# Scan steps over four head pairs, with the first scores and the first substitution placed in the value projection

## The chip, the cores and the metric

One core of one Trainium2 chip runs the whole program. The metric is the device time in microseconds, the median of several runs. Its engines are named as in the profile: PE is TensorE, DVE is VectorE, ACT is ScalarE, POOL is GpSimd and SP is SyncE, which issues most transfers.

## What is computed

A decoder of two layers over 512 tokens of width 1024, in fp32. Layer A is RWKV-7 time mixing, layer B differential attention; each is followed by a squared-ReLU MLP and a gated per-layer embedding. The change concerns only the recurrence of layer A, over 16 heads of 64:

```python
def step(S, inp):
    r_t, w_t, k_t, v_t, a_t, b_t = inp
    Sa = jnp.einsum('bhvk,bhk->bhv', S, a_t)
    S = S * w_t[:, :, None, :] + Sa[..., None] * b_t[:, :, None, :] + v_t[..., None] * k_t[:, :, None, :]
    y = jnp.einsum('bhvk,bhk->bhv', S, r_t)
    return S, y
...
r = xr @ w_rkvo[0]
k = xk @ w_rkvo[1]
v = xv @ w_rkvo[2]
```

The kernel computes it in chunks of 64 tokens. Within a chunk the dependence of a token on earlier ones is a lower triangular system; it is inverted in blocks of 32 and applied as a matmul, and only a 64x64 state per head goes from chunk to chunk.

## The kernel before

**Dense parts.** Every fp32 weight is split into a high part (ScalarE, `high`) and a low part (GpSimd, `low`, line 419), and each product is three matmuls (`three`, lines 572 to 574). Weights come in blocks of 256 columns through two slots of `wraw`, `whi` and `wlo`. Blocks 0 to 3 of the twelve projection blocks `N_K + t` are the keys, 4 to 7 the receptances, 8 to 11 the values; a block is eight steps of six matmuls. Functions in `hooks` run ahead of a chosen step of a block.

**Units.** A unit is one head pair (a 128-row tile of channels, c = 0 to 7) in one chunk: 8 x 8 = 64 units, in 16 groups q of four. Before, a group is two head pairs by two chunks (`units_of`). NQ is 16 and HALF is 8. For each group:
- the scores with the decayed a-side (`b_score`, line 703): ScalarE puts the a-tiles of two heads on the diagonal of a 128-wide tile (`early_copies`, line 1280), TensorE multiplies, and for groups 0 to 7 VectorE masks the result into NL (`scored`, line 1795), for groups 8 to 15 ScalarE takes it raw (`raw_scores`, line 1331) and GpSimd masks it (line 498);
- GpSimd spreads Bbd, Kbd and Vbd (line 459), TensorE transposes them (`turn`, line 715), ScalarE takes them to Btok, Ktok and Vtok (line 1341);
- `k_score` (line 729) gives the local scores LL, which VectorE masks (line 1848);
- the 32-blocks of eight groups at a time are inverted by a recursion of 30 steps on VectorE, two passes each (lines 1804 to 1824), and the corner block by two matmuls (`lower_times` line 740, `corner` line 749) with Nbd (line 472), Xbd (line 1858) and TiT (lines 485 and 1871).

**Scan.** Two interleaved lines x = 0 and 1. One step of a line, for one unit: `values_in` (767), `state_in` (776), Zt on VectorE (1879), its transposition `z_turn` (784), Zs on ScalarE (1355), `solve` (791), Us on ScalarE (1361), `keys_in` (799), `answer` (806, 809), the new state Hs on VectorE (1890, 1893), the decayed state Hg on ScalarE (1348), the output on ScalarE (1366). There are 32 steps. The preparation of group q + 1 is cut into eight pieces (`fill`) that are written by hand between the matmuls of two steps.

**What sets the order.** All is written by hand: each engine executes its list in order and waits on semaphores. The first eight groups' inverse runs ahead of the scan; that of the other eight (`inverse_part(1, k)`) is threaded into the first 13 steps, three recursion steps at a time between `state(1, k - 1)` and Zt of x = 1. VectorE starts the whole stage after `pe_step` 8 x 16, the end of the value projection.

Of the kernel before, what the change touches and what calls it, by code (L numbers as in the profile page):

```python
# [25 lines left out]
P = 128  # L26
# [7 lines left out]
CH = 64  # L34
# [20 lines left out]
C_ROW = C_LOW + CH  # L55
C_TRS = C_ROW + 8
# [11 lines left out]
def shape_constants():  # L68
# [8 lines left out]
    c[:, C_ROW] = (i // BL) % 2  # L77
# [50 lines left out]
def trunk(nc, x, p, norm_g, mlp_w1, mlp_w2, ple_w_up, ple_w_gate, rwkv_mix, rwkv_w_rkvo, rwkv_w0, rwkv_w1,  # L128
# [5 lines left out]
    with ctx:  # L134
# [4 lines left out]
        def at(name, offset, shape, dtype=F32):  # L139
# [6 lines left out]
        ST, HIDH, HIDL, RSTD, TMP, CST = 98432, 180352, 186496, 192640, 194688, 202880  # L146
# [46 lines left out]
        inv_t = at("inv_t", W_HI + 10240, [P, BL, BL])  # L193
        inv_p = at("inv_p", W_HI + 14336, [P, 256])
        inv_d = [at("inv_d0", W_LO, [P, NB, BL]), at("inv_d1", W_LO + 34816, [P, NB, BL])]
        inv_dt = [at("inv_dt0", W_LO + 4096, [P, NB, BL]), at("inv_dt1", W_LO + 38912, [P, NB, BL])]
# [4 lines left out]
        Zt = [at(f"Zt{k}", REST + 4096 + 512 * k, [P, P]) for k in range(2)]  # L201
        Hg = [at(f"Hg{k}", REST + 5120 + 512 * k, [P, P]) for k in range(2)]
        assert REST + 6144 <= XX
        Zs = [at(f"Zs{k}", HIDH + 512 * k, [P, P]) for k in range(2)]
        Us = [at(f"Us{k}", HIDH + 1024 + 512 * k, [P, P]) for k in range(2)]
        Hs = [at(f"Hs{k}", HIDL + 1024 * k, [P, 2, P]) for k in range(2)]
        Bbd = at("Bbd", TMP, [P, QUAD, P])
        Kbd = at("Kbd", TMP + 2048, [P, QUAD, P])
        Vbd = at("Vbd", TMP + 4096, [P, QUAD, P])

# [29 lines left out]
        row2 = cst[:, C_ROW:C_ROW + 1]  # L240
# [5 lines left out]
            bd_zero bb_pre bs_mm nl_ev nl_raw nl_mask inv_lk inv_d bbd kbd vbd nbd tdg  # L246
# [25 lines left out]
        def units_of(q):  # L272

            return 2 * (q // 4), (q % 4) * P

        def chunk_of(x, k):

            return 2 * (k // 8) + x, slice((k % 8) * CH, (k % 8 + 1) * CH)

        def states(k):  # L280

            return k - k // 8 + 1

        def kept(k):

            return 6 * (k // 8) + k % 8
# [11 lines left out]
        def _(sp):  # L298
# [74 lines left out]
            for k in range(2):  # L373
                sp.wait_ge(s.y_mm[k], NQ)
            for t in range(TT):
                sp.dma_start(xtok2[:, t, :], x[0, t * P:(t + 1) * P, :]).then_inc(s.x2_in, 16)
            slot_free(N_G2)
# [27 lines left out]
        def _(pool):  # L405
# [34 lines left out]
            lows(N_K, N_V + 4)  # L440
# [1785 lines left out]
```

## Time and profile before

| | us |
|---|---|
| median of 3 runs (1749.82 to 1750.33) | 1750.26 |
| profiled execution | 1748.08 |
| its span | 1746.2 |
| TensorE busy | 1608.3 (92%) |
| VectorE busy | 788.6 (45%) |
| ScalarE busy | 636.1 (36%) |
| GpSimd busy | 638.5 (37%) |

The profile is one execution taken by the hardware profiler. Its windows give busy time by stage, its list of waits who was waited for, its timeline single instructions with start and length. Times in the text count from the start of the span. The scan and its preparation lie between 256 and 489 us.

### The profile page before, as it was taken

What the parts mean: (1) busy time and instruction counts of PE and PEld (TensorE: products, weight loads), DVE (VectorE), ACT (ScalarE), POOL (GpSimd) and SP (SyncE); (2) the same over time, 40 slices, a digit from 0 to 9 for tenths busy, and PEclk for the clock granted to TensorE, in tenths of its full rate; (3) what the DMA queues carried; (4) which work ended last, traced back from release to release, by engine and by line L of the source; (5) the groups of instructions that cost most, each with busy time, mean ns of one, the idle gap of its engine ahead of it and who ended that gap; (6) DMA issues with size and microseconds to landing.
All of it is one profiled execution on the core that took longest, in us unless ns stands there. A gap on an engine that the chain in (4) does not pass through costs nothing. (4 is left out here: it accounts for less than half of the span.)

```text
span 1746.2 us, 20826 instructions
## 1 busy us (share of the span) xinstructions
PE 1608.3 (92%) x7503; PEld 1276.4 (73%) x7503; DVE 788.6 (45%) x1241; ACT 636.1 (36%) x1063; POOL 638.5 (37%) x309
## 2 busy tenths in 40 slices
PE   4799993879989999999999979998899999999998
PEld 3566683879937878888887767765567888888877
DVE  4866948673345532013213767357545320132133
ACT  4655433445543422122224343336724221122242
POOL 4233233334322344434433425352223343344442
PEclk8899996899989999999999999998999999999999
DMA  4112200002011233322223233220002223322221
GB/s 129 58 63 73 72 25 0 2 15 98 2 48 37 84 96 101 104 96 96 96 97 103 83 112 97 73 72 25 1 24 97 96 96 108 96 96 97 96 80 65
DMA packets 123462, 127.17 MB, mean 73 GB/s; under 512 B 8316, under 2 KB 120060, under 8 KB 123384
## 3 DMA queue, kind: packets, MB, share of 16 engines
q1 hardware_dynamic: 122720, 124.90, 21.9%
q8 instruction: 48, 0.79, 0.2%
q0 software_dynamic: 288, 0.63, 0.2%
q10 hardware_dynamic: 376, 0.61, 0.1%
q14 instruction: 30, 0.25, 0.0%
HBM read 124.00 MB, written 2.12 MB: 72 GB/s over the span
## 5 line engine op out<-in xcount | busy, mean ns | idle before, releaser
L419 POOL TENSOR_TENSOR wlo<-wraw,whi 128x2048 fp32r<-128x2048 f32 (+1 forms) x111 | 506.6, 4564 | 866.4 <-ACT whi L1167 796.2
L572 PE MATMUL pb<-xh,whi 128*128 128x512 f32 x1184 | 476.2, 402 | 27.2 <-DVE xl L1669 14.6
L573 PE MATMUL pb<-xl,whi 128*128 128x512 f32 x1184 | 465.7, 393 | 0.0
L574 PE MATMUL pb<-xh,wlo 128*128 128x512 f32 x1184 | 465.5, 393 | 0.0
L572 PEld LDWEIGHTS pb<-xh,whi 128*128 128x128 f32 x1184 | 224.7, 190 | 101.0 <-issue 38.1
L1167 ACT ACTIVATE whi<-wraw 128x2048 fp32r<-128x2048 f32 (+1 forms) x111 | 209.2, 1884 | 235.7 <-PE pb L574 235.5
L573 PEld LDWEIGHTS pb<-xl,whi 128*128 128x128 f32 x1184 | 225.2, 190 | 48.0 <-issue 3.4
L574 PEld LDWEIGHTS pb<-xh,wlo 128*128 128x128 f32 x1184 | 225.0, 190 | 47.7
L572 PE MATMUL pb<-hid_h,whi 128*128 128x512 f32 x512 | 202.4, 395 | 0.0
L574 PE MATMUL pb<-hid_h,wlo 128*128 128x512 f32 x512 | 202.3, 395 | 0.0
L573 PE MATMUL pb<-hid_l,whi 128*128 128x512 f32 x512 | 202.3, 395 | 0.0
L1980 DVE TENSOR_TENSOR X<-X,pb 128x512 f32<-128x512 f32 x40 | 25.7, 683 | 297.2 <-PE pb L574 297.2
L2012 DVE TENSOR_TENSOR tmp<-pb,rstd 128x512 f32<-128x512 f32 x64 | 41.2, 686 | 208.4 <-PE pb L574 207.9
L1465 ACT ACTIVATE hid_h<-tmp 128x512 f32 (+1 forms) x64 | 39.6, 633 | 251.1 <-DVE tmp L2016 251.1
L572 PEld LDWEIGHTS pb<-hid_h,whi 128*128 128x128 f32 x512 | 96.2, 188 | 23.1
L573 PEld LDWEIGHTS pb<-hid_l,whi 128*128 128x128 f32 x512 | 96.3, 188 | 23.0
L574 PEld LDWEIGHTS pb<-hid_h,wlo 128*128 128x128 f32 x512 | 96.2, 188 | 23.0
L1435 ACT ACTIVATE tmp<-X 128x512 f32<-128x512 f32 x40 | 24.3, 628 | 128.4 <-DVE X L1980 123.6
L1985 DVE SCALAR_TENSOR_TENSOR xl<-X,PV,xh 128x512 fp32r<-128x512 f32 x48 | 52.7, 1159 | 28.9 <-ACT xh L1176 28.9
L1174 ACT ACTIVATE xh<-tmp 128x512 fp32r<-128x512 f32 x64 | 40.1, 633 | 61.3 <-DVE tmp L1680 28.4
L1669 DVE TENSOR_TENSOR xl<-tmp,xh 128x512 fp32r<-128x512 f32 x64 | 51.2, 810 | 23.4 <-ACT xh L1174 23.4
L2082 DVE RECIPROCAL tmp<-tmp 128x512 f32<-128x512 f32 x12 | 40.2, 3346 | 23.9 <-ACT tmp L1540 23.9
(275 smaller groups left out, 2032.3 us busy)
## 6 DMA issues: line engine op xcount, KB each, us to landing
wraw<-in_mlp_w_dram SPq DMA_DIRECT2D x128, 512.0 KB, 4.3
wraw<-in_rwkv_w_rkvo_dram SPq DMA_DIRECT2D x32, 512.0 KB, 4.4
wraw<-in_ple_w_gate_dram SPq DMA_DIRECT2D x16, 512.0 KB, 4.4
xtok<-in_x_dram SPq DMA_DIRECT2D x8, 512.0 KB, 6.0
wraw<-in_w_k_shared_dram SPq DMA_DIRECT2D x8, 512.0 KB, 4.0
wraw<-in_w_v_shared_dram SPq DMA_DIRECT2D x8, 512.0 KB, 4.4
wraw<-in_diff_w_q_dram SPq DMA_DIRECT2D x8, 512.0 KB, 4.0
wraw<-in_diff_w_o_dram SPq DMA_DIRECT2D x8, 512.0 KB, 4.4
```

The lines of the kernel that those rows point to most:

```text
L419: pool.tensor_tensor(wlo[:, par, rng], wraw[:, par, rng], whi[:, par, rng].bitcast(F32), ALU.subtract).then_inc(s.w_lo, 1)
L572: mm(o, wh, ah, start=first, stop=False)
L573: mm(o, wh, al, start=False, stop=False)
L574: return mm(o, wl, ah, start=False, stop=last)
L1167: A(whi[:, par, rng], wraw[:, par, rng], ACT.Copy).then_inc(s.w_hi, 1)
L1174: A(xh[:, k, :], src, ACT.Copy).then_inc(s.x_hi, 1)
L1465: A(hid_h[:, bass.ds(4 * i + 2 * h + m, 1), :], tmp[:, 2 + m:3 + m, :], ACT.Copy)\
L1669: tt(xl[:, k, :], src, xh[:, k, :].bitcast(F32), ALU.subtract).then_inc(s.x_ready, 1)
L1980: tt(X[:, c, 0:S], X[:, c, 0:S] if old is None else old, b, ALU.add).then_inc(sem, 1)
L1985: stt(xl[:, k, :], X[:, k, 0:S], vec(k, gain), xh[:, k, :].bitcast(F32), ALU.mult, ALU.subtract)\
L2012: tt(tmp[:, m, :], pb[2 * h + m][:, :], rstd[:, :], ALU.mult).then_inc(s.dense_v, 1)
L2082: dve.reciprocal(tmp[:, i % 2, :], tmp[:, i % 2, :]).then_inc(s.qk_rs, 1)
```

## The change

- A group is now four head pairs of one chunk, and one scan step takes a whole group: line x has the head pairs 2x and 2x + 1, both in one bank of PSUM, each instruction of VectorE or ScalarE on Zt, Zs, Us and the output takes both. There are 16 steps.
- Score groups 0 to 9 are computed by hooks in blocks 9, 10 and 11 of the projections, on own tiles `early`; ScalarE takes all of them raw, between its evacuations. Score groups 10 to 15 are written between the pieces of the preparation of group 0. The mask of the half that gives answers moves to GpSimd, one pass per group (`mask_answers`), that of the other half into three passes ahead of each inverse (`block_pieces`).
- VectorE's substitution for groups 0 to 7 waits for eight raw scores and for the low part of the last but one value block, no longer for the end of the projection. Its tiles lie in the slots of `wraw`, so the load of the next weight waits for them.
- The second half's recursion is threaded in by single steps, four parts per scan step, in steps 0 to 7.
- `low` of a 2048-wide weight block is two instructions of 1024.
- The stage buffer ST and those behind it lie 384 bytes higher.

```diff
         def units_of(q):
-            return 2 * (q // 4), (q % 4) * P
+            return QUAD * (q // HALF), slice((q % HALF) * CH, (q % HALF + 1) * CH)
...
             def low(n, par, rng, first):
...
+                if rng.stop == 2048:
+                    front = slice(0, 1024)
+                    pool.tensor_tensor(wlo[:, par, front], wraw[:, par, front], whi[:, par, front].bitcast(F32),
+                                       ALU.subtract)
+                    rng = slice(1024, 2048)
...
-                     5: {5: kk_spread(3)}, 6: {6: kk_spread(4), 7: kk_spread(5)}, 7: {1: kk_spread(6)}, 8: {4: kk_spread(7)}}
+                     5: {5: kk_spread(3)}, 6: {6: kk_spread(4), 7: kk_spread(5)}, 7: {1: kk_spread(6)}, 8: {4: kk_spread(7)},
+                     9: {1: two_scores(0), 5: two_scores(2)}, 10: {1: two_scores(4), 5: two_scores(6)}, 11: {5: two_scores(8)}}
...
             def solve(x, k):
                 pe.wait_ge(s.z_ev[x], k + 1)
-                if k % 2 == 0:
-                    pe.wait_ge(s.tt_ev, 2 * (k // 2) + 2)
-                mm(pb[CB[x]][:, 0:P], set_at(x, k)[4], Zs[x][:, :], start=True, stop=True).then_inc(s.u_mm[x], 1)
+                pe.wait_ge(s.tt_ev, 2 * k + 2)
+                for i in range(2):
+                    ins = mm(pb[CB[x]][:, half_of(i)], set_at(x, i, k)[4], Zs[x][:, i, :], start=True, stop=True)
+                ins.then_inc(s.u_mm[x], 1)
...
             for t in range(12):
                 n = N_K + t
-                if t == 11:
-                    act.wait_ge(s.prep, CT)
-                    act.wait_ge(s.bd_zero, 3)
+                if t == 9:
+                    act.wait_ge(s.prep, QUAD)
+                    act.wait_ge(s.dense_v, QUAD)
+                    act.wait_ge(s.x_ready, X_V + CT)
                     early_copies(0)
                     early_copies(1)
+                if 9 <= t < 11:
+                    q = 4 * (t - 9)
+                    for m in range(q, q + 4):
+                        raw_scores(m)
+                        early_copies(m + 2)
...
-            dve.wait_ge(s.pe_step, 8 * N_G2)
-
             lk = Link(dve, s.inv_lk)
...
+            def block_pieces(hf, i):
+
+                if i == 0:
+                    dve.wait_ge(s.nl_raw, HALF * (hf + 1))
+                    if hf == 0:
+                        dve.wait_ge(s.w_lo, N_V + 3)
+                    lk.mark(tt(inv_s[hf][:, :, :], NL[hf][:, :, 0:BL], dg_a, ALU.mult))
+                elif i == 1:
+                    lk(tt(inv_d[hf][:, :, :], NL[hf][:, :, BL:CH], dg_b, ALU.mult))
...
+            LATE = ((1, 2, 3), (4, 5)) + tuple((j,) for j in range(6, 27)) + ((27, 28), (29, 30))
...
+            def mask_answers(q):
+
+                pool.wait_ge(s.nl_raw, q + 1)
+                lrb = NL[q // HALF][:, QUAD * (q % HALF):QUAD * (q % HALF + 1), CH:P]
+                pool.tensor_tensor(lrb, lrb, tri_r, ALU.mult).then_inc(s.nl_mask, 1)
+                pool.wait_ge(s.nl_mask, q + 1)
```

TensorE at the end of the projections. Before, the score groups follow the last matmul of block 11 (L574); L703 is a score group, L715 a transposition.

```order
L574 MATMUL pb<-xh,wlo 128x512
L703 MATMUL pb<-St,Bbd 128x128 x4
L703 MATMUL pb<-St,Kbd 128x128 x4
L703 MATMUL pb<-St,Bbd 128x128 x4
L703 MATMUL pb<-St,Kbd 128x128 x4
```

After, two groups (L704) stand between the matmuls of a block (L596 to L598), here for the first time in block 9.

```order
L597 MATMUL pb<-xl,whi 128x512
L598 MATMUL pb<-xh,wlo 128x512
L704 MATMUL pb<-St,early_106 128x128 x4
L704 MATMUL pb<-St,early_107 128x128 x4
L596 MATMUL pb<-xh,whi 128x512
```

Ten of sixteen groups have moved ahead of the projection's end. Next, VectorE in the scan's first half. Before, six recursion passes (L1816, L1818) stand ahead of Zt of x = 1 (L1879); L1893 is a state, L1848 the local scores.

```order
L1893 SCALAR_TENSOR_TENSOR Hs_101<-pb,small,Hg_95 128x128
L1816 TENSOR_TENSOR inv_p<-inv_d_85,inv_t 128x210
L1818 TENSOR_TENSOR inv_t<-inv_t,inv_p 128x21x10
L1816 TENSOR_TENSOR inv_p<-inv_d_85,inv_t 128x220
L1818 TENSOR_TENSOR inv_t<-inv_t,inv_p 128x20x11
L1816 TENSOR_TENSOR inv_p<-inv_d_85,inv_t 128x228
L1818 TENSOR_TENSOR inv_t<-inv_t,inv_p 128x19x12
L1858 TENSOR_TENSOR Xbd<-pb,cst 128x8x32
L1879 TENSOR_TENSOR Zt_93<-pb,cst 128x128
```

After, for the same recursion steps: L1877 and L1879 are the recursion's two passes, L1909 the local scores, L1940 Zt, L1959 the states.

```order
L1932 TENSOR_TENSOR TiT_76<-TiT_76,pb 64x4x32 x2
L1940 TENSOR_TENSOR Zt_95<-pb,cst 128x256
L1877 TENSOR_TENSOR inv_p<-inv_d_85,inv_t 128x210
L1879 TENSOR_TENSOR inv_t<-inv_t,inv_p 128x21x10
L1959 SCALAR_TENSOR_TENSOR Hs_94<-pb,small,Hg_102 128x128 x2
L1877 TENSOR_TENSOR inv_p<-inv_d_85,inv_t 128x220
L1879 TENSOR_TENSOR inv_t<-inv_t,inv_p 128x20x11
L1909 TENSOR_TENSOR LL_77<-pb,cst 128x512
L1940 TENSOR_TENSOR Zt_96<-pb,cst 128x256
```

One recursion step of two passes now stands between any two pieces of the scan. On GpSimd a group in the scan had these rows before (spreads L459, Nbd L472, diagonal blocks L485).

```order
L459 COPY Bbd<-St 64x4x64 x2
L459 COPY Kbd<-St 64x4x64 x2
L472 TENSOR_TENSOR Nbd<-NL_88,cst 128x8x32
L459 COPY Vbd<-St 64x4x64 x2
L485 TENSOR_TENSOR TiT_76<-inv_dt_86,cst 128x512
```

After, the mask of the answers (L510) is added behind the diagonal blocks.

```order
L478 COPY Bbd<-St 64x4x64 x2
L478 COPY Kbd<-St 64x4x64 x2
L487 TENSOR_TENSOR Nbd<-NL_89,cst 128x8x32
L478 COPY Vbd<-St 64x4x64 x2
L500 TENSOR_TENSOR TiT_76<-inv_dt_86,cst 128x512
L510 TENSOR_TENSOR NL_89<-NL_89,cst 128x4x64
```

Per group it is one pass more, and two passes in a row that read two inputs.

## Rows read from the trace of the kernel before

**Rows 1.** Windows: us, busy by engine (instructions), granted clock, DMA share, GB/s.

```profile
213.00:256.00 43.00, 42.51 (x186) 34.10 (x185) 22.09 (x24) 12.19 (x17) 15.25 (x6) 1.00 0.08 25
...
279.00:303.00 24.00, 3.60 (x16) 3.06 (x15) 22.25 (x54) 1.19 (x2) 1.31 (x4) 0.50 0.00 0
308.00:395.00 87.00, 70.49 (x550) 67.73 (x550) 59.66 (x142) 35.50 (x116) 31.22 (x52) 0.93 0.03 8
395.00:480.00 85.00, 84.37 (x733) 82.71 (x732) 33.33 (x99) 45.60 (x155) 33.75 (x61) 0.99 0.14 51
```

**Rows 2.** Waits of TensorE over the span: us in total, times, longest.

```profile
PE pb L740 <- DVE LL L1848: 20.8, 1, 20.8
...
PE pb L784 <- DVE Zt L1879: 16.4, 12, 2.4
```

**Rows 3.** Timeline, VectorE: start, length, instruction; local scores of groups 0, 1, 8, 15.

```profile
302.65 0.70 DVE L1848 TENSOR_TENSOR LL<-pb,cst 128x512 f32<-128x512 f32 x1
...
312.45 0.68 DVE L1848 TENSOR_TENSOR LL<-pb,cst 128x512 f32<-128x512 f32 x1
...
404.63 0.69 DVE L1848 TENSOR_TENSOR LL<-pb,cst 128x512 f32<-128x512 f32 x1 [0.15 <-PE pb L729]
...
472.49 0.69 DVE L1848 TENSOR_TENSOR LL<-pb,cst 128x512 f32<-128x512 f32 x1 [0.16 <-PE pb L729]
```

**Rows 4.** Timeline, ScalarE: the scan's last output.

```profile
489.08 0.22 ACT L1366 ACTIVATE St<-pb 128x64 f32<-128x64 f32 x1 [0.53 <-PE pb L809]
```

**Rows 5.** Timeline of VectorE and GpSimd: the first substitution, and copies beside it.

```profile
264.95 2.01 DVE L1804 SCALAR_TENSOR_TENSOR inv_t<-NL,cst 128x1024 f32<-128x1024 f32 x1
...
278.40 0.44 DVE L1816 TENSOR_TENSOR inv_p<-inv_d,inv_t 128x130 f32<-128x130 f32 x1
...
280.63 0.33 DVE L1816 TENSOR_TENSOR inv_p<-inv_d,inv_t 128x168 f32<-128x168 f32 x1
...
299.06 2.02 DVE L1822 STREAM_TRANSPOSE inv_d<-inv_t 128x1024 f32<-128x1024 f32 x1
...
277.86 0.85 POOL L459 COPY Bbd<-St 64x256 f32<-64x256 f32 x2
```

**Rows 6.** Timeline, ScalarE in the value projection: evacuations (L1299) and a weight copy.

```profile
222.51 1.09 ACT L1299 ACTIVATE St<-pb 128x512 f32<-128x512 f32 x2 [4.46 <-PE pb L574]
223.48 1.92 ACT L1167 ACTIVATE whi<-wraw 128x2048 fp32r<-128x2048 f32 x1
...
245.03 1.09 ACT L1299 ACTIVATE St<-pb 128x512 f32<-128x512 f32 x2 [7.99 <-PE pb L574]
...
255.92 1.08 ACT L1299 ACTIVATE St<-pb 128x512 f32<-128x512 f32 x2 [8.19 <-PE pb L574]
```

**Rows 7.** Timeline, TensorE: first and last of the 16 score groups.

```profile
255.72 1.06 PE L703 MATMUL pb<-St,Bbd 128*128 128x128 f32 x8
...
274.46 1.16 PE L703 MATMUL pb<-St,Kbd 128*128 128x128 f32 x8 [0.34 <-ACT Kbd L1280]
```

**Rows 8.** Timeline, TensorE: two pieces of one unit in the second half.

```profile
471.18 0.39 PE L799 MATMUL pb<-Vtok,Ktok 128*128 128x128 f32 x2
471.40 0.39 PE L767 MATMUL pb<-LL,Vtok 128*128 128x128 f32 x2
```

**Rows 9.** Groups by shape, 300 to 490 us: count, busy us, mean ns, idle before.

```profile
L485 POOL TENSOR_TENSOR TiT<-inv_dt,cst 128x512 f32<-128x512 f32 x16 | 20.6, 1290 | 67.5 <-PE pb L809 44.9 <-DVE inv_dt L1824 22.5
...
L1879 DVE TENSOR_TENSOR Zt<-pb,cst 128x128 f32<-128x128 f32 x64 | 18.6, 290 | 52.0 <-PE pb L776 43.4 <-PE pb L767 8.4
...
L1355 ACT ACTIVATE Zs<-pb 128x128 f32<-128x128 f32 x64 | 17.7, 276 | 29.2 <-PE pb L784 29.0
```

**Rows 10.** Timeline, TensorE: a transposition of Zt that waited.

```profile
353.54 0.33 PE L784 MATMUL pb<-cst,Zt 128*128 128x128 f32 x1 [1.95 <-DVE Zt L1879]
```

**Rows 11.** Timeline: a pass of VectorE beside a low part, and TensorE behind it.

```profile
1017.11 4.66 DVE L1977 TENSOR_TENSOR tmp<-tmp 128x512 f32<-128x512 f32 x1 [1.52 <-ACT tmp L1435]
...
1023.36 2.04 PE L605 MATMUL pb<-tmp,cst 128*128 128x512 f32 x2 [6.73 <-DVE tmp L1977]
```

More of the change, by code:

```diff
@@ L209, in trunk @@
         Vbd = at("Vbd", TMP + 4096, [P, QUAD, P])
+        early = [at("early0", CST + 4 * C_END + 4 * CT * NV + 896, [P, QUAD, P]), at("early1", RSTD, [P, QUAD, P])]
         hid_h = at("hid_h", ST, [P, 16, S], F32R)
@@ L438, in lows @@
                         low(n0 + 2 * i + h, (n0 + h) % 2, slice(0, 2048), False)
-            lows(N_K, N_V + 4)
+            pool.memset(early[0][:, :, :], 0.0).then_inc(s.bd_zero, 1)
+            lows(N_K, N_V + 2)
+            pool.wait_ge(s.kb_ps, CT)
+            pool.memset(early[1][:, :, :], 0.0).then_inc(s.bd_zero, 1)
+            lows(N_V + 2, N_V + 4)
             link = Link(pool, s.pool_link)
@@ L507, in _ @@
                 spread(Kbd, K_, q, s.kbd)
-                lower_block(q)
                 if q:
+                    lower_block(q)
                     pool.wait_ge(s.tr_mm, 3 * q)
-                    spread(Vbd, V_, q, s.vbd)
+                else:
+                    pool.wait_ge(s.inv_ld, 1)
+                    pool.memset(Vbd[:, :, :], 0.0).then_inc(s.bd_zero, 1)
+                    pool.wait_ge(s.pe_step, 8 * N_G2)
+                    for t in (Xbd, Nbd):
+                        pool.memset(t[:, :, :], 0.0).then_inc(s.bd_zero, 1)
+                    pool.wait_ge(s.bd_zero, 7)
+                    pool.wait_ge(s.dense_a, 36)
+                spread(Vbd, V_, q, s.vbd)
+                if q == 0:
+                    lower_block(q)
                 diagonal_blocks(q)
+                mask_answers(q)
             for k in range(2):
-                pool.wait_ge(s.y_mm[k], 2 * NQ - 2)
+                pool.wait_ge(s.y_mm[k], NQ - 1)
             low(N_G2, 0, slice(0, 2048), False)
             for k in range(2):
-                pool.wait_ge(s.y_mm[k], 2 * NQ)
+                pool.wait_ge(s.y_mm[k], NQ)
             low(N_WO, 1, slice(0, 2048), False)
@@ L811, in fill @@
+                pe.wait_ge(s.nl_mask, k + 1)
+                for i in range(2):
+                    lrb = NL[k // HALF][:, QUAD * (k % HALF) + 2 * x + i, CH:P]
+                    ins = mm(pb[ZY[x]][:, i * P + CH:(i + 1) * P], Us[x][:, i, :], lrb, start=False, stop=True,
+                             skip_group_check=True)
+                ins.then_inc(s.y_mm[x], 1)
             def fill(q, slot):
@@ L816, in fill @@
                     turn(q, 0)
+                    k_score(q, 0, 2)
                 elif slot == 1:
[L818 removed]
+                    k_score(q, 2, 4)
+                    turn(q, 1)
                 elif slot == 2:
[L820 to L827 removed]
+                    lower_times(q, 0, 4)
+                else:
                     turn(q, 2)
[L829 removed]
                     corner(q)
[L832 to L835 removed]
+            b_score(10)()
+            b_score(11)()
+            fill(0, 0)
+            b_score(12)()
+            b_score(13)()
+            fill(0, 1)
+            b_score(14)()
+            b_score(15)()
+            fill(0, 2)
+            fill(0, 3)
             values_in(0, 0)
[L837 to L839 removed]
+            for k in range(NQ + 1):
+                if k < NQ:
                     state_in(0, k)
@@ L843, in _ @@
                     keys_in(1, k - 1)
-                fill(q, f)
-                if k < 2 * NQ:
+                fill(k + 1, 0)
+                if k < NQ:
                     z_turn(0, k)
@@ L848, in _ @@
                     answer(1, k - 1)
-                fill(q, f + 1)
-                if k < 2 * NQ:
+                fill(k + 1, 1)
+                if k < NQ:
                     solve(0, k)
```

434 lines of the change are left out of this document (221 added, 213 removed).

## The prediction

> **What bounds the kernel now.** I read the stages of the span first (the windows), then who made TensorE wait, then the timelines of single engines. Over the whole span TensorE is the engine that sets the time, except in the stage this change rewrites, the chunked scan of the RWKV layer and its preparation. From 213 to 256 us, the value projection, TensorE is busy 42.5 of 43 us; from 279 to 303 us it is busy 3.6 of 24 us at a granted clock of 0.50 while VectorE is busy 22.3; from 308 to 395 us it is busy 70.5 of 87; from 395 to 480 us it is busy 84.4 of 85 [rows 1]. The two largest waits in this stage are the one of 20.8 us for the local scores LL, which stand on VectorE behind the first-half substitution, and 16.4 us in twelve pieces for Zt [rows 2]. So three prices are to be worked out: when the scan can start, what a group of four units costs in its first half (where VectorE still carries the second substitution) and in its second half, and the tail.
>
> How the scan now runs. LL(q) marks the groups: LL(1) at 312.45, LL(8) at 404.63, LL(15) at 472.49 [rows 3]. Seven groups of the first half take 92.18 us, 13.2 each; seven of the second take 67.86, 9.69 each. The last output copy ends 0.22 us after its start at 489.08, so at 489.3 [rows 4]; from LL(15) to there are 16.8 us.
>
> **Start of the scan.** Before, VectorE begins the first-half substitution at 264.95 and LL(0) stands at 302.65, 37.7 us later [rows 3, 5]. It could begin only when the value projection was over (its last evacuation is at 255.92 [rows 6]) and the first eight score groups were out. The change computes score groups 0 to 9 inside blocks 9 to 11 of the projections.
> - TensorE: a score group is 8 passes in about 0.9 us (8 x 0.11, the same kind as in rows 8; 1.06 with the last one's drain [rows 7]). Block 9 starts when block 8 ends, 222.45. Its hook at the second of eight steps (1.36 us each, a block of 10.9 us by the distance of two evacuations, 245.03 to 255.92) comes at 223.8, but the first copy into the early tile stands on ScalarE behind the evacuation at 222.51 and the weight copy at 223.48, which ends at 225.40 [rows 6], and takes 0.85. TensorE waits until 226.2, 2.4 us. Then four groups, 3.6 us: block 9 ends at 239.3. Block 10 has four groups and ends at 253.8, block 11 two groups and ends at 266.5 instead of 255.9. This delay of the projection, 10.6 us, is paid by taking ten groups out of the 16 that now stand behind it (255.72 to 275.6 [rows 7]).
> - ScalarE turns each group over in 0.60 + 0.85 us; raw score 7 is out at 250.9. By then the low part of the last weight has left GpSimd (ScalarE's copy until 242.3, then an instruction as long as the 4.66 us hold of rows 11: 247), so VectorE starts at 250.9, 14.0 us earlier.
> - The substitution itself: three passes of 1024 elements replace the one of 2.01 us: 1.25 + 1.25 + 2.2; then transposition 1.25, copy 0.7, ones 0.1 come to 6.8. Steps 7 to 30 took 18.4 us undisturbed (280.63 to 299.06 [rows 5]), steps 1 to 6 have the lengths of the last six and take 3.5 by them. Before, from 264.95 to step 7 at 280.63 it was 15.7 us, since GpSimd masked the second half against VectorE; now this part is 6.8 + 3.5, and GpSimd has only memsets and one spread of Vbd there, for which I put 1.5. The two last transpositions are 3.6. Sum 33.9: LL(0) at 284.8, 17.9 us earlier.
> - From LL(0) to the first Zt it was 5.8 us; now three passes for the second half (1.25, 1.25, 2.2) are threaded between, against diagonal and mask work on GpSimd; I take 9.2, so Zt at 294.0. TensorE works in this stretch at the low clock as it did in the 0.50 stretch before [rows 1], since it still waits some 6 us for LL(0). The first step has more of VectorE's work (transposition, copy, three and two recursion steps); LL(1) comes at 296.5 and the next step begins at 302.3. LL(1) is **16.0 us earlier** than 312.45.
>
> **A group in the second half.** The count of matmul passes per four units does not change: 12 transpositions, 24 passes of scores, lower blocks and corner, and 13 for each unit, 88 in all. Two full passes follow each other in 0.22 us [rows 8], so 72 x 0.112 + 16 x 0.09 = 9.5 us; a group now takes 10.0 (9.69 plus the two chunk ends, 1.1 us shorter each, among the seven). The rest is short waits at the head of the scan's matmuls. With two head pairs in one step there are half as many of them. Chain of one pair of heads per step: state_in 0.45, Zt 0.42 (0.29 for 128 elements, 0.69 for 512 [rows 9, 3]), transposition 0.35, Zs 0.39 (0.28 for 128 [rows 9]), solve 0.55, Us 0.39, answer 0.55, two states 0.70, eight hand-overs of 0.05: 4.2 us, well inside 9.7, and between any two links of it TensorE has 0.9 to 2.1 us of other work. The corner and Vtok are the tightest (0.9 us of corner over a copy of 0.6). I take **9.7**; bounds 9.5 and 10.0.
>
> **A group in the first half.** Three recursion steps in a row stood before one Zt: in one instance TensorE waited 1.95 us for Zt [rows 10]. Now one step (0.8 us) stands between two links. By my hand schedule of one step, from state_in(0) at 0: Zt(0) 0.74 to 1.16 with its transposition due at 2.2; states(1) until 3.8; the next recursion step meets GpSimd's diagonal pass (1.29 [rows 9]) and the new mask (half the elements, 0.7), both released at 3.3, and ends at 6.1; LL 6.8 where the lower blocks wanted it at 5.84: TensorE waits 1.0; the rest hides. 9.5 + 1.0 = **10.5**. Bounds: 9.7 (no collision counts) and 13.3, what it is now with the chunk end added back. The last recursion step and the two transpositions of the second half add 1.0 once.
>
> LL(1) to LL(15) is then 11.9 (first step) + 6 x 10.5 + the seventh step's rest and 6 x 9.7 with the chunk end of four units (-2.2) and +1.0, together 141.3 us, against 160.0: **-18.7**. Tail: LL(15) sits 5.0 us into its step, so 4.7 remain, and the last step is one chain of each x plus the wait behind the weight copy of 1.90 us that also stands there now: 7.2. 11.9 against 16.8: **-4.9**.
>
> **Low parts in halves.** GpSimd's long instructions hold VectorE: a 0.69 us pass took 4.66 at 1017.11, and TensorE then waited 6.73 us [rows 11]. In halves each hold is at most 2.3, but the second half comes right behind and meets the next VectorE pass, so I count only the one pass that slips between, 0.5 us at each of the two places where TensorE waits for it: **-1.0**. Elsewhere TensorE works through 10.9 us blocks and neither the hold nor the 0.1 us of a second instruction reaches the end; without that cover 100 such pairs would cost 10 us.
> The Trainium skill (SBUF — State Buffer, "Who interferes with whom") says that an instruction of VectorE with two SBUF inputs and one of GpSimd that reads SBUF exclude each other for the whole of an instruction; the 4.66 us row agrees with it. By that rule alone a hold would shrink by 2.3 us at each of the two places, -4.6 instead of -1.0. The tile shifts and the 384 bytes cost nothing.
>
> **Sum.** -16.0 - 18.7 - 4.9 - 1.0 = -40.6. The profiled execution took 1748.08 us (span 1746.2), 2.2 under the median: 1750.26 - 40.6 = **1710**.
>
> **Rivals.**
> - *The first half keeps its waits.* VectorE's order is still fixed; if every recursion step runs into GpSimd, a step stays at 13.3: 7 x 2.8 = +20, 1730. For it: GpSimd has 0.7 us more per group, and by the counts above VectorE's own work is 7.3 us, 9 with the holds. Against: single steps instead of three. 12%.
> - *GpSimd's copies block too.* The six spreads of 0.43 us per group could hold VectorE as the two-input passes do: +1.0 on a step by two more holds, 1717. Against: a pass of VectorE ran in 0.44 us beside such copies [rows 5]. This is what the skill's rule on that page would give, since a copy reads SBUF. 12%.
> - *Serial chains, slower.* If solve, copy and answer of both x no longer hide each other, because each link waits for two units' work, a step is 2 x 4.2 + 5.6 us of fill = 14.0: 7 x 3.5 + 7 x 4.3 = +55, 1765. It decides against the change from 12.8 us a step on. Against: the 84.4 of 85 us busy with shorter links. 5%.
> - *The early start fails.* Hooks stall on the copies of ScalarE in all three blocks, or VectorE starts only after the projection (267): +14, 1724. 6%.
> - Forecast: 65%.
>
> **Numbers.** The forecast's own bounds: 14 steps by -0.2 or +0.3 and -0.8 (first half), the start +-3: 1700 to 1716. Up to the first rival it is 1730; below 1700 and above 1728 I leave about 2 in 10. A measurement of this kernel can tell 0.2%, 3.5 us, from no change. Faster 0.94, same 0.01, slower 0.05.
>
> **What would show it.** LL(0) near 285, first Zt near 294, LL(1) to LL(8) about 10.5 apart, LL(8) to LL(15) 9.7, the projection ending at 266, the last output copy at 450. Waits for Zt should go from 16.4 to a few us, waits for LL before the lower blocks should appear, about 1 us each. Wrong would be: steps of 12 or more in the first half (rival one), or a TensorE wait over 3 us at the hooks of blocks 10 and 11.

## The result, and the profile after

The median fell from 1750.04 to 1694.99 us (four runs each; ratio 0.9688, 95% interval 0.9671 to 0.9705). That is 55 us where I had forecast 40.6, and below the low end of the range, 1700. The profiled executions took 1748.08 and 1695.06 us, their spans 1746.2 and 1693.2: 53.0 us. One remark is needed for the numbers below: the times of one kernel lie up to 9.6 us apart (before: 1741.86 to 1751.45 in 23 runs), and what differs between them is how long the granted clock of TensorE was low (mean clock 0.967 to 0.971 in the runs of before below 1744 us, 0.963 to 0.967 in those above 1749). So I give medians for the verdicts and traces for the places.

Windows of after, columns as in [rows 1]: the value projection, the substitution up to the first Zt, and the two halves of the scan.

```profile
213.00:256.00 43.00, 40.92 (x209) 33.61 (x208) 25.45 (x26) 22.16 (x38) 18.50 (x14) 1.00 0.08 25
266.00:290.00 24.00, 15.01 (x96) 13.97 (x95) 21.81 (x43) 9.70 (x20) 8.70 (x10) 0.72 0.00 1
293.00:375.00 82.00, 76.84 (x663) 74.19 (x661) 61.02 (x140) 33.15 (x91) 40.37 (x71) 1.00 0.03 9
375.00:437.00 62.00, 60.30 (x530) 58.97 (x528) 22.59 (x61) 27.82 (x77) 30.97 (x55) 1.00 0.19 69
```

The stretch in which VectorE works alone is still there, but TensorE now does 15 of its 24 us instead of 3.6, and in the first half of the scan it is busy 77 of 82 us where it was 70.5 of 87. The waits of TensorE in after answer to [rows 2]; columns: us in total, times, longest.

```profile
PE pb L772 <- DVE LL L1909: 8.3, 1, 8.3
...
PE pb L629 <- DVE tmp L2056: 5.8, 1, 5.8
...
PE pb L748 <- ACT Btok L1401: 3.8, 14, 0.3
...
PE pb L704 <- ACT early L1329: 1.9, 3, 1.2
...
PE pb L854 <- ACT Us L1421: 1.4, 1, 1.4
```

The 20.8 us for LL are 8.3, the 16.4 for Zt are 0.5. New are 14 short waits of 0.27 us for the copy of Btok. The timeline of VectorE in after: the start of the substitution, and the local scores of groups 0, 1, 8 and 15 (as [rows 3]).

```profile
249.27 1.23 DVE L1856 TENSOR_TENSOR inv_s<-NL,cst 128x1024 f32<-128x1024 f32 x1 [17.14 <-ACT NL L1334]
...
282.14 0.70 DVE L1909 TENSOR_TENSOR LL<-pb,cst 128x512 f32<-128x512 f32 x1
...
293.45 0.69 DVE L1909 TENSOR_TENSOR LL<-pb,cst 128x512 f32<-128x512 f32 x1
...
367.62 0.69 DVE L1909 TENSOR_TENSOR LL<-pb,cst 128x512 f32<-128x512 f32 x1 [0.28 <-PE pb L761]
...
436.95 0.69 DVE L1909 TENSOR_TENSOR LL<-pb,cst 128x512 f32<-128x512 f32 x1 [0.28 <-PE pb L761]
```

The last output copy of the scan (as [rows 4]), and the two last links ahead of it on TensorE:

```profile
448.91 0.71 PE L831 MATMUL pb<-Zs,TiT 128*128 128x128 f32 x4 [0.47 <-ACT Zs L1415]
450.98 1.12 PE L854 MATMUL pb<-NL,Us 128*128 128x64 f32 x4 [1.36 <-ACT Us L1421]
...
452.13 0.28 ACT L1426 ACTIVATE St<-pb 128x128 f32<-128x128 f32 x1 [1.21 <-PE pb L854]
```

Where the 53.0 us come from, by the start of the same instruction in both timelines:

| same instruction | before | after | offset | in this piece | forecast |
|---|---|---|---|---|---|
| weight copy behind block 8 | 223.48 | 221.26 | -2.2 | -2.2 | 0 |
| LL(1) | 312.45 | 293.45 | -19.0 | -16.8 | -16.0 |
| LL(15) | 472.49 | 436.95 | -35.5 | -16.5 | -18.7 |
| last output copy of the scan | 489.08 | 452.13 | -37.0 | -1.4 | -4.9 |
| a matmul of the group norm | 499.78 | 462.06 | -37.7 | -0.8 | 0 |
| one behind the norm's root | 526.64 | 486.05 | -40.6 | -2.9 | 0 |
| ahead of the first MLP's hidden rows | 631.40 | 590.96 | -40.4 | +0.2 | 0 |
| behind them | 943.11 | 897.63 | -45.5 | -5.0 | 0 |
| end of the attention projections | 1170.87 | 1124.45 | -46.4 | -0.9 | -1.0 |
| in the attention | 1234.40 | 1185.27 | -49.1 | -2.7 | 0 |
| at the second MLP's hidden rows | 1414.65 | 1365.77 | -48.9 | +0.2 | 0 |
| near the end | 1703.20 | 1649.57 | -53.6 | -4.7 | 0 |

The scan and its preparation (three rows of forecasts) gave 34.7 us instead of 39.6. Within it only the first half gained: LL(1) to LL(8) took 92.2 us and takes 74.2, LL(8) to LL(15) took 67.9 and takes 69.3. Not all of the 18.0 need be the change's: before has three stretches of 3.4 us at the low clock in that half (from 332.0, 345.7 and 393.5), after has none, and the same scan took between 88.4 and 92.2 us in the traces of the other kernels that keep it (b_stage384, b_stage128).

The excess lies behind the scan, in code of which the change touches no line but the halves, and comes in two kinds. The first is in both MLPs. Groups of instructions over the span, matmuls with the hidden activations; us busy, mean ns of one; first before, then after:

```profile
L572 PE MATMUL pb<-hid_h,whi 128*128 128x512 f32 x512 | 202.4, 395 | 0.0
L574 PE MATMUL pb<-hid_h,wlo 128*128 128x512 f32 x512 | 202.3, 395 | 0.0
```

```profile
L596 PE MATMUL pb<-hid_h,whi 128*128 128x512 f32 x512 | 199.4, 389 | 0.0
L598 PE MATMUL pb<-hid_h,wlo 128*128 128x512 f32 x512 | 199.2, 389 | 0.0
```

The 6 ns are a difference of start to start as well. Timeline of TensorE, seven matmuls apart; before 1.40 us for six, after 1.37:

```profile
1439.61 0.40 PE L574 MATMUL pb<-hid_h,wlo 128*128 128x512 f32 x1
...
1441.01 0.40 PE L574 MATMUL pb<-hid_h,wlo 128*128 128x512 f32 x1
```

```profile
1439.66 0.39 PE L598 MATMUL pb<-hid_h,wlo 128*128 128x512 f32 x1
...
1441.03 0.39 PE L598 MATMUL pb<-hid_h,wlo 128*128 128x512 f32 x1
```

Over all 1536 of them the mean distance is 233.2 and 226.8 ns: 9.8 us. The second kind is the clock. Windows behind a gap of the group norm and in the attention (granted clock is the third number from the end), before, then after, same code:

```profile
519.90:526.60 6.70, 6.07 (x13) 3.90 (x14) 2.77 (x4) 1.17 (x2) 0.00 (x0) 0.50 0.00 0
1183.00:1192.00 9.00, 8.48 (x23) 5.22 (x24) 5.67 (x16) 4.39 (x17) 1.87 (x3) 0.50 0.13 44
```

```profile
482.70:486.10 3.40, 3.28 (x14) 2.19 (x14) 2.01 (x4) 0.00 (x0) 0.00 (x0) 1.00 0.00 0
...
1136.00:1140.00 4.00, 2.76 (x10) 1.96 (x10) 3.63 (x6) 2.77 (x10) 0.66 (x1) 0.57 0.49 168
1140.00:1146.00 6.00, 6.00 (x30) 3.49 (x29) 5.32 (x16) 4.25 (x14) 1.21 (x2) 1.00 0.00 1
```

Behind the group norm the low stretch (6.8 us before) is absent; in the attention 10.2 us of it have become 3.4.

### The profile page after: what moved, and what is told of

The parts are those of the page before. It is cut to its first block and busy times, and to the rows that moved or that the text cites. A ratio compares the mean times of both kernels' runs of the same rounds, so it can differ in the third digit from the quotient of the medians.

```text
span 1693.2 us, 20697 instructions
## 1 busy us (share of the span) xinstructions
PE 1581.9 (93%) x7503; PEld 1264.5 (75%) x7503; DVE 773.1 (46%) x1205; ACT 624.3 (37%) x975; POOL 666.1 (39%) x427
## 5 line engine op out<-in xcount | busy, mean ns | idle before, releaser
L435 POOL TENSOR_TENSOR wlo<-wraw,whi 128x1024 fp32r<-128x1024 f32 x108 | 260.7, 2414 | 807.3 <-ACT whi L1214 752.2
L596 PE MATMUL pb<-xh,whi 128*128 128x512 f32 x1184 | 476.4, 402 | 28.6 <-DVE xl L1729 16.2
L598 PE MATMUL pb<-xh,wlo 128*128 128x512 f32 x1184 | 464.9, 393 | 0.0
L596 PEld LDWEIGHTS pb<-xh,whi 128*128 128x128 f32 x1184 | 224.6, 190 | 103.1 <-issue 42.0
L438 POOL TENSOR_TENSOR wlo<-wraw,whi 128x1024 fp32r<-128x1024 f32 x111 | 274.3, 2471 | 20.8 <-ACT whi L1214 20.8
L598 PEld LDWEIGHTS pb<-xh,wlo 128*128 128x128 f32 x1184 | 224.7, 190 | 47.8
L596 PE MATMUL pb<-hid_h,whi 128*128 128x512 f32 x512 | 199.4, 389 | 0.0
L598 PE MATMUL pb<-hid_h,wlo 128*128 128x512 f32 x512 | 199.2, 389 | 0.0
L598 PEld LDWEIGHTS pb<-hid_h,wlo 128*128 128x128 f32 x512 | 96.1, 188 | 20.1
L596 PEld LDWEIGHTS pb<-hid_h,whi 128*128 128x128 f32 x512 | 96.1, 188 | 19.6
```

Source lines behind the costliest of these rows:

```text
L435: pool.tensor_tensor(wlo[:, par, front], wraw[:, par, front], whi[:, par, front].bitcast(F32), ALU.subtract)
L596: mm(o, wh, ah, start=first, stop=False)
L598: return mm(o, wl, ah, start=False, stop=last)
```

## Experiments

**Undo the side changes and do them alone.** Theory A: the start address of the stage buffer sets how fast TensorE reads the hidden activations. Theory B: the halves of the low parts do it, and the 384 bytes do nothing, as I had written.

```diff
-        ST, HIDH, HIDL, RSTD, TMP, CST = 98432, 180352, 186496, 192640, 194688, 202880
+        ST, HIDH, HIDL, RSTD, TMP, CST = 98816, 180736, 186880, 193024, 195072, 203264
```

In before alone:

> Kernel before with only the six tiles from the stage buffer on moved up by 384 bytes; nothing else. Theory A (where the stage buffer starts sets how fast TensorE reads the hidden activations): the 1536 matmuls that read hid_h and hid_l stand 233.2 ns apart before and 226.8 after, so 1536 x 6.4 ns = 9.8 us less, and about 0.3 us from the low-rank ones: near 1740. The waits of the scan (20.8 us for LL, 16.4 for Zt) stay. Theory B, that of my prediction (the shift costs and brings nothing; the faster spacing comes from halves of the low parts): 1750, spacing unchanged.

Measured 1740.52 (12 runs; ratio to before 0.9957, interval 0.9938 to 0.9976): -9.8, with the distance at 226.8. The clock did not help: its median over the runs is 0.963, against 0.966 of before. The reverse in after:

> Kernel after with the six tiles put back by 384 bytes. Theory A: +10 us, 1705, the hidden matmuls 233 ns apart again, and the scan as in after (LL(1) 293.4, LL(15) 437, last output copy 452). Theory B: 1695. The two places where the granted clock was about 0.5 before and 1.00 after (520 to 527 and 1183 to 1192 us before) are watched: if the clock there has to do with when they come, the first one keeps its clock here, since nothing ahead of it moves, and the second may change.

Measured 1702.20: +4.5 to +7.2 against the two medians of after (1697.71 and 1694.99); the distance is 233.2 again. The traces tell more than these medians. The span is 8.2 us longer than that of after: the hidden rows of the two MLPs give back some 10 us by the offsets (4.7 and 5.2), and 2.3 are regained between 950 and 1080 us, where the two kernels' stretches at the low clock differ. The mean clock over the runs is a little higher as well (0.980, against 0.974 to 0.978 in those of after). The scan is as in after. Of the two places that were watched, the first keeps its full clock and the second has 3.4 us at the low one, both as in after. Theory B falls: the spacing follows the address in both directions.

**Which address.** Before with two other shifts, one run each (1742.02 and 1749.71 us; the spacing is what is compared).

```diff
-        ST, HIDH, HIDL, RSTD, TMP, CST = 98432, 180352, 186496, 192640, 194688, 202880
+        ST, HIDH, HIDL, RSTD, TMP, CST = 98560, 180480, 186624, 192768, 194816, 203008
```

> Kernel before with the six tiles up by 128 bytes in place of 384. The tile xh, whose matmuls stand 228 ns apart, starts a whole number of 512 bytes from the slab's start; the hidden tiles of before start 128 bytes past such a place, those of after on one, these 256 past one. If 256 bytes are the step that counts: spacing of the hidden matmuls 227 ns as in after. If it is 512: 233 ns as before, or something between. If any other place than that of before is good (a clash with one certain other tile): 227. One look; the spacing is read from the trace.

> Kernel before with the six tiles up by 256 bytes: 384 bytes past a multiple of 512. If steps of 256 or 512 bytes count: 233 ns. If any other place than that of before is good: 227 ns.

Groups of instructions, up by 128 bytes, then up by 256:

```profile
L572 PE MATMUL pb<-hid_h,whi 128*128 128x512 f32 x512 | 199.3, 389 | 0.0
```

```profile
L572 PE MATMUL pb<-hid_h,whi 128*128 128x512 f32 x512 | 202.3, 395 | 0.0
```

Distances 226.8 and 233.0 ns. So at 0 and 256 bytes past a multiple of 512 from the slab's start the reading is fast, at 128 and 384 it is slow: among the four places tried, multiples of 256 are good.

**Halves alone, and whole parts in after.**

```diff
+                if rng.stop == 2048:
+                    front = slice(0, 1024)
+                    pool.tensor_tensor(wlo[:, par, front], wraw[:, par, front], whi[:, par, front].bitcast(F32),
+                                       ALU.subtract)
+                    rng = slice(1024, 2048)
```

> Kernel before with only the low weight parts computed in two instructions of 1024 columns in place of one of 2048. Theory A: the spacing of the hidden matmuls stays at 233 ns; the gain is what the trace of after shows at the places where TensorE or VectorE stands behind GpSimd: 2.2 us between 180 and 221 us and 0.9 at 1023, so -3, near 1747. My prediction's term: -1.0, 1749. By the rule of a lock for a whole instruction at each of two places: -4.6, 1745.5. Theory B (halves make the spacing shorter): -12 or more, 1738.

> Kernel after with the low weight parts in whole instructions again. If halves are worth the same as alone in before, about +3: 1698. If the new order of the scan's preparation leans on them (VectorE works against GpSimd's low parts from 249 to 256 us), +4 to +6: 1700. By my prediction's term: +1.0, 1696.

Alone: 1740.72 (ratio 0.9955, interval 0.9938 to 0.9973), -9.6, more than the terms of 1.0, 3 and 4.6; and since the hidden matmuls stay 233.2 ns apart, Theory B falls here too. After without the halves: 1701.45, +3.7 to +6.5, also more than the 1.0 of my prediction. VectorE in before at the two places, first the clamp ahead of the key norm's reciprocal (here GpSimd works from 182.57 to 187.56), then the place of [rows 11]:

```profile
184.44 3.40 DVE L1734 TENSOR_SCALAR rstd<-rstd 128x512 f32<-128x512 f32 x1 [1.35 <-ACT rstd L1260]
...
1017.11 4.66 DVE L1977 TENSOR_TENSOR tmp<-tmp 128x512 f32<-128x512 f32 x1 [1.52 <-ACT tmp L1435]
...
1022.52 0.69 DVE L1977 TENSOR_TENSOR tmp<-tmp 128x512 f32<-128x512 f32 x1 [0.76 <-ACT tmp L1435]
```

With halves:

```profile
184.34 1.18 DVE L1739 TENSOR_SCALAR rstd<-rstd 128x512 f32<-128x512 f32 x1 [1.36 <-ACT rstd L1265]
...
1007.93 2.50 DVE L1982 TENSOR_TENSOR tmp<-tmp 128x512 f32<-128x512 f32 x1 [1.52 <-ACT tmp L1440]
...
1011.19 1.99 DVE L1982 TENSOR_TENSOR tmp<-tmp 128x512 f32<-128x512 f32 x1 [0.76 <-ACT tmp L1440]
```

At the place of [rows 11] the mechanism of my step holds: the first hold shrinks by 2.2, the next pass, free before, is now held 1.3, and 1.0 us is left (the wait of 6.7 becomes 5.7), where my sum had 0.5. A hold of the same length 20 us earlier (at 997.01 in before) gives nothing: its 4.77 becomes 2.56, the next pass goes from 0.68 to 2.88, and TensorE's wait behind them stays at 2.1. At the clamp the whole 2.2 us come through: TensorE's wait for that reciprocal fell from 2.7 to 0.5. Even so the 1.18 us are not free of the first half, which ends at 185.24: the same clamp takes 0.42 at 152.64 in before, where GpSimd is idle. The rest is between 1000 and 1130 us of before (990 to 1120 here), where TensorE's waits for xl fell from 6.7 us in four to 4.7 in three and one of 0.8 is gone, against two new ones of 0.3 for low parts. By offsets 2.6 us are gained up to 223 us (in it a new wait of 0.8 us for a low part, and one stretch at the low clock less) and 2.7 between 1000 and 1130 us, together 5.3. The rest of the 9.6 goes with the clock: its median over the runs is 0.971, against 0.966 of before. Whether the halves bring that about is not shown.

The reason that the expectation had for +4 to +6 in after, that the new scan leans on the halves, does not hold: the trace without them is 2.1 us behind after at 212 us and still 2.1 behind at LL(15).

The Trainium skill (SBUF — State Buffer, "Who interferes with whom") calls the hold exclusive for a whole instruction, and lists `tensor_scalar`, the clamp's operation, among those that can take the shared ports with a single input; the 3.40 us that became 1.18 agree with that where the next instruction of VectorE takes no second input from SBUF, and at the other place the second half's hold takes most of it back.

**Both together, scan as before.**

> Kernel before with both side changes: tiles up by 384 bytes and low parts in halves; the scan as before. If the two add up by the medians of the single runs (-9.8 and -9.6): 1731. By the offsets of the traces, leaving out the stretches at the low clock (-9.8 and about -6): 1734. What is left to after, 36 to 39 us, is then the scan's and its preparation's, against the 39.6 of my prediction for these.

Measured 1732.89 (ratio 0.9908, interval 0.9887 to 0.9929): -17.2. The next run, timed together with it, takes after as it is:

> Kernel after unchanged, timed with the others of this call. The runs of the kernels so far fall into two heaps some 8 us apart (before: 1742 and 1750.5), each stretch at the low clock costing TensorE 1.7 to 3.4 us. If that belongs to every variant, after has a second heap too, near 1703 or 1687; if the new scan has left fewer waits that let the clock fall, all runs stay within 2 us of 1695.

1697.71, from 1695.86 to 1700.02 in 5 runs: not 8 us apart as before is, but not within 2 either. 35.2 us by the medians are thus the new scan with its preparation, against the forecast of 39.6.

**The early scores put back behind the projection** (ScalarE's copies move with them).

```diff
-                     9: {1: two_scores(0), 5: two_scores(2)}, 10: {1: two_scores(4), 5: two_scores(6)}, 11: {5: two_scores(8)}}
...
+            for q in range(0, HALF + 2, 2):
+                two_scores(q)()
```

> Kernel after with the ten score groups taken out of blocks 9 to 11 of the projections and put behind the projection, with their ScalarE copies; all else as in after. Then the substitution starts after the projection (256) and eight score groups at ScalarE's pace of 1.45 us, near 268 in place of 249.3, and TensorE no longer loses 10.6 us in the projection. Theory: LL(1) 17 to 18 us later, 1712. Rival (what the early start gives is taken back by something else, as the two transpositions and the second half's masks): +10 or less, under 1705.

Measured 1719.49, timed together with the 1697.71 of after, so +21.8 (spans of the traces +18.2). VectorE's start and TensorE's wait in this kernel:

```profile
267.95 1.22 DVE L1850 TENSOR_TENSOR inv_s<-NL,cst 128x1024 f32<-128x1024 f32 x1 [37.42 <-ACT NL L1335]
```

```profile
PE pb L773 <- DVE LL L1903: 22.2, 1, 22.2
```

The start is 18.7 us later than 249.27 and nothing behind it takes that back. Of the 35.2 us this leaves 13 to 17 for all the rest of the new scan, the steps of four head pairs, the threading and the masks together; no kernel with the steps alone taken out was run.

**Recursion steps in threes.** My reason for the shorter first half was that one recursion step, no longer three, stands ahead of a Zt.

```diff
                     local_scores(k + 1)
+                    if k:
+                        for i in range(4 * k - 2, 4 * k + 1):
+                            inverse_late(i)
                     z_spread(1, k)
...
-                    inverse_late(4 * k)
```

> Kernel after with the second substitution's steps of a scan step put together again: three in a row ahead of the second Zt (as before the change), one behind the states, in place of four single ones between the links. My prediction ascribes the waits of TensorE for Zt in the first half (16.4 us in 12 before) to this grouping: three steps of 0.8 us in a row put each Zt some 1.6 us late, six to seven steps of the scan: +8 to +11 us on the 10.65 us period (12 and more), about 1706. Rival: two head pairs per step give TensorE enough other work beside each Zt, and the grouping does not matter: within 2 us of 1697, period 10.7.

Measured 1697.08, as after (1697.71 and 1694.99, neither timed together with it). LL comes every 10.58 us (303.71 to 346.01 in four groups) against 10.65. Window 316 to 345 us of this kernel, then of after, and this kernel's waits for Zt:

```profile
316.00:345.00 29.00, 28.02 (x245) 27.24 (x244) 20.21 (x50) 12.10 (x34) 14.12 (x25) 1.00 0.01 1
```

```profile
316.00:345.00 29.00, 28.01 (x244) 27.14 (x243) 21.34 (x51) 11.48 (x32) 13.35 (x24) 1.00 0.01 1
```

```profile
PE pb L823 <- DVE Zt L1940: 1.9, 3, 1.2
```

Within those 29 us TensorE is busy 28 in both. In these steps the grouping costs nothing: the waits for Zt are 0.1 to 0.2 us each. Only at 360.8 us does TensorE wait 1.2 for a Zt, and a stretch of 3.4 us at the low clock follows; with it LL(1) to LL(8) takes 75.7 us against 74.2. That the second head pair gives TensorE the work that covers three recursion steps is the likely reason; no run separates it. So it is not the single steps that took the waits for Zt away, as I had it.

**The second half.** A group takes 10.29 us (385.51 to 436.95 in five), more than before's 10.0. TensorE and ScalarE of after in one such group: the copy of Btok starts behind the answers (L854), which have nothing to do with it.

```profile
415.28 0.56 PE L854 MATMUL pb<-NL,Us 128*128 128x64 f32 x4
415.68 0.66 PE L761 MATMUL pb<-St,Kbd 128*128 128x128 f32 x4
416.61 0.66 PE L748 MATMUL pb<-cst,Kbd 128*128 128x128 f32 x4 [0.27 <-ACT Btok L1401]
```

```profile
415.96 0.60 ACT L1401 ACTIVATE Btok<-pb 128x512 f32<-128x512 f32 x1 [2.09 <-PE pb L854]
```

ScalarE waits for `y_mm`, since the set is free only when its last reader is done; of Btok itself the last reader is the matmul ahead (L848, `h_mm`).

```diff
                 if q >= 2 and i == 0:
-                    act.wait_ge(s.y_mm[0], q - 1)
-                    act.wait_ge(s.y_mm[1], q - 1)
+                    for x in range(2):
+                        act.wait_ge(s.h_mm[x], q - 1 - (q - 1) // HALF)
```

> Kernel after with two waits of ScalarE changed. (1) Its copy of the turned Bbd into Btok waits for the matmuls that read the old Btok, no longer for the answers behind them (0.45 us later). TensorE waits 0.27 us per group for that copy, 14 times, 3.8 us in all: -3.8 if that wait is what keeps the group at 10.29 where I had forecast 9.7. (2) The weight copy of 1.90 us at the end of the scan goes behind the last Us copy: TensorE waited 1.36 us there: -1.4. Sum -5, about 1690. Rival: another link takes the wait's place (the period stays above 10.2): -1.4 alone, 1693.6. If the period comes to 10.0, not 9.7, it is TensorE's own 88 passes that set it.

Measured 1694.98, timed together with the 1697.71 of after: -2.7. The Btok wait is gone from the list; LL comes every 9.89 us (387.99 to 437.46 in five), and TensorE is busy all of those 49.47 us. The wait for the last Us went from 1.36 to 0.47. The 88 passes alone thus take 9.9, where I had 9.5 and 0.2 for waits.

The first half did not get shorter: its groups stay at 10.6 to 10.7 us although TensorE no longer waits for Btok there. In its place TensorE waits 0.45 to 0.58 us in each of five groups ahead of the lower blocks (L772). The profile names no releaser ("issue"), but each of these waits ends 0.1 us after LL does (LL starts at 347.73 and takes 0.69). In after the same waits are there, behind those for Btok: 0.06 to 0.17 us in five groups, 0.87 in the seventh.

```profile
348.53 1.05 PE L772 MATMUL pb<-inv_d,Nbd 128*128 128x32 f32 x8 [0.47 <-issue]
```

What is still lacking in the sum is partly clock. The profiled run is one of the two slowest of five (1698.55). By offsets against the second trace of after its scan gains 0.8 us, and a fall of the clock takes 3.0 in it; without that fall the two waits give 3.9 of the 5. In the seventh group TensorE had stood 0.27 and later 0.87 us in after; here it stands 1.27 at once, for LL(7), and the clock falls, as it does in the next kernel, which has the same pause. The row of this kernel, then its window:

```profile
359.93 1.05 PE L772 MATMUL pb<-inv_d,Nbd 128*128 128x32 f32 x8 [1.27 <-issue]
```

```profile
361.70:368.50 6.80, 6.80 (x35) 6.80 (x35) 5.09 (x7) 1.59 (x4) 0.93 (x3) 0.52 0.00 1
```

**Is it the standing that lets the clock fall?** In all 13 other traces, before's included, the clock falls in two waits of TensorE. Here they are filled with work that nothing reads, where TensorE waits 5.8 us for a norm's sum and 4.3 us for the head norms:

```diff
+                for _ in range(n):
+                    mm(pb[bank][:, :], ones, cst[:, 0:S], start=True, stop=True)
...
+                busy(7, 6)
                 norm_total(4)
...
+            pe.wait_ge(s.lg, 64)
+            busy(0, 4)
```

> The kernel with the two changed waits of ScalarE (1695.0 median, period 10.02), and added work that nothing reads: six 128x512 matmuls of constants on TensorE where it waits 5.8 us for the key norm (976 us in after), four where it waits 4.3 us for the head norms (1216 us). In both places the granted clock then falls to 0.50 for 6.8 us, while TensorE has full work. Theory: the clock falls because TensorE stood idle; with the gap filled it stays at 1.00 there, and each place gives 3.4 us less the small delay of the fillers: -6, 1689 (against 1695.0 of that kernel). Rival: the clock falls anyway, or somewhere else soon after: 1695 or up to 2 us over it.

Measured 1689.00 (1686.94 to 1692.84; ratio to before 0.9666, interval 0.9643 to 0.9688): -6.0 against the 1694.98 of the kernel it is built on (not timed together; before had 1750.08 beside the one and 1750.04 beside the other), and faster than both before and after. Windows over the two gaps, with the added work, then in the second trace of after:

```profile
970.00:983.00 13.00, 12.46 (x43) 7.70 (x42) 8.02 (x4) 3.42 (x5) 8.62 (x3) 1.00 0.32 93
1211.00:1225.00 14.00, 12.77 (x35) 6.16 (x36) 9.76 (x11) 5.59 (x8) 0.00 (x0) 1.00 0.00 1
```

```profile
971.00:984.00 13.00, 7.12 (x17) 4.72 (x16) 6.52 (x3) 3.93 (x5) 8.60 (x3) 0.74 0.28 90
1212.00:1227.00 15.00, 9.47 (x29) 4.74 (x29) 5.76 (x5) 4.91 (x7) 0.00 (x0) 0.77 0.00 0
```

Each of the two falls is gone. By the starts of the same instructions this kernel leads that trace by 1.6 us at 978 and by 4.5 at 990, by 4.5 at 1200 and by 6.8 at 1228: 2.9 and 2.3 us. In these two places the clock fell because TensorE stood, and keeping it busy with work that nothing reads gives the time back. The other falls stay: those at 361.7 and 959.1 us, for instance, are in this trace as in that of the kernel it is built on (362.0 and 962.8).

## Why the prediction was wrong, point by point

- **The stage buffer.** The step that failed first: "the tile shifts and the 384 bytes cost nothing". I asked only what a shift could break, found nothing, and put down zero on both sides. It is worth 9.8 us by the spacing (233.2 to 226.8 ns, 1536 times), seen in both directions. That alone would have moved the forecast to 1700. All six tiles moved together in every such run; the spacing that was compared is that of the matmuls which read the hidden activations. The profile of before held the hint: by groups, the same shape of matmul took 395 ns with hid_h and hid_l and 389 with xl and wlo in the same MLP.
- **The low clock behind the scan.** The sum carried the stretches of before at the low clock along as if they belonged to the code. One of them was absent in after and one was shorter, 2.9 and 2.7 us, and the medians differ by 2 us more than the two profiled executions. These are not shown to be the change's: the same wait of 2.9 us ahead of the group norm is followed by a fall in before and in the kernel with the two changed waits, and by none in after, in its second trace and in the kernel with the added work. The range had no term for it.
- **Halves.** -1.0 was sized for two places at 0.5. The place of [rows 11] alone gave 1.0 and the hold at 997 us nothing; the key norm's clamp (2.2) and the other waits between 1000 and 1130 us were not looked for. After against after with whole parts is 3.7 to 6.5 us; the Trainium skill's rule at two places, -4.6, was nearer in size, though not for its reason.
- **Start of the scan.** Right in mechanism and size: -16.8 against -16.0, and 18.7 us when undone. In detail, the hook of block 9 stalled 1.2 us, not 2.4; VectorE began at 249.3 (forecast 250.9), LL(0) came at 282.1 (284.8), LL(1) at 293.5 (296.5). Of these leads 2.2 us were there before block 9, from the halves (the two traces spend the same 31 us at the low clock up to 210 us, in different pieces). The parts listed for LL(0) add to 33.8, not 33.9.
- **First half.** 10.65 against 10.5. The term for LL had the right mechanism: TensorE does wait for LL ahead of the lower blocks, about 0.5 us instead of 1.0 once the wait for Btok is gone (in after 0.1 behind Btok's 0.27), and taking the wait for Btok away did not shorten these groups. But what is left of a group is 10.1 to 10.3 us, where I had 9.5, so that 10.5 came so near is luck. My reason for the end of the waits for Zt was wrong: with three recursion steps in a row the period is 10.58.
- **Second half.** 10.29 against 9.7, outside my bounds of 9.5 to 10.0 and the reason why LL(1) to LL(15) gave 16.5 and not 18.7. The passes take 9.9 (forecast 9.5 plus 0.2), the other 0.3 to 0.4 is the wait of ScalarE on a semaphore that says more than is needed. My chain per head pair had all its own links; of the copies of the preparation, which share ScalarE and one PSUM bank with each other, I had priced only that of Vtok.
- **Tail.** -1.4 against -4.9. From LL(15) 6.3 us remained of its step (forecast 4.7) and the last step took 9.2 (7.2): the weight copy of 1.90 us, which I had counted in, stands ahead of the last Us, and TensorE waits 1.36 for it. In the kernel that moves it behind, the tail is about 1 us shorter; what else makes up the 3.5 us is open.
- **Rivals.** None came at its price: the waits for Zt went from 16.4 us to 0.5, the period is 10.65 and not 11.5, 13.3 or 14, and VectorE began at 249.3. But the mechanism of the second rival is there, and I had misread the row against it. The pass of 0.44 us beside the copies of [rows 5] (130 elements, 278.40) takes 0.30 alone (328.12 in before). In after, a pass of 30 elements alone, then beside a copy:

```profile
278.11 0.19 DVE L1877 TENSOR_TENSOR inv_p<-inv_d,inv_t 128x30 f32<-128x30 f32 x1
...
293.88 0.85 POOL L478 COPY Bbd<-St 64x256 f32<-64x256 f32 x2
...
294.39 0.38 DVE L1877 TENSOR_TENSOR inv_p<-inv_d,inv_t 128x30 f32<-128x30 f32 x1
```

The copies thus hold such passes, by about 0.1 to 0.25 us each. What that costs a group was not measured.

## What to carry over

When tiles move, compare the spacing of equal matmuls by tile before believing that an address is free; at the four places tried here, a moving operand on a multiple of 256 bytes was read faster. When a step's waits vanish, look at what each semaphore says beyond what its reader needs, since a shared "all done" count turns into the next wait. Where a wait is taken away and the period stays, look for the wait behind it, also among those that the profile puts down to "issue". And take the stretches at the low clock out of both traces before adding up terms: they cost about 1 to 3 us each here, change from run to run, and a gap of TensorE that can't be closed can be filled.

## What the runs showed of the hardware

- TensorE's reading of a 128x512 fp32 moving operand depends on its start address: 226.8 ns from start to start at 0 or 256 bytes past a multiple of 512 (from the slab's start), 233.0 at 128 or 384. The Trainium skill (SBUF — State Buffer, "Operand start alignment") asks only for a multiple of the element size, which all four have, and says that this is about legality and not speed; the runs add the price.
- The granted clock fell to about 0.5 during waits of TensorE of 5.7 to 6.7 and of 4.3 us, in all 13 traces that have them unfilled, and it stayed at 1.00 in both places in the one trace where unused matmuls fill them. Shorter waits do not decide it: the clock also fell in the scan after one wait of 1.24 to 1.27 us (three traces), and did not fall at the same place after 0.27 and 0.87 us apart, nor after one of 1.27 us at 264.5 in after; a wait of 2.9 us was followed by a fall in some traces and by none in others. The Trainium skill (TensorE: Matmul & The Clock Gate, "HAM oscillation — how this bites in real kernels") describes kernels whose waits throttle the next work; that unused matmuls in the wait avoid it is what the last run shows.
- One instruction of GpSimd on 2048 columns held a VectorE pass with a single input for 3.40 us. Beside halves it takes 1.18, and 0.42 where GpSimd is idle.
- Copies of 0.43 us by GpSimd hold passes of VectorE with two inputs: a pass of 30 columns takes 0.38 us beside one and 0.19 alone.
